# Stick-breaking attention: the later-key sums and the mask as single-pass products of exact constants with high and low parts of the softplus rows

## The chip, the cores and the metric

The kernel runs on one core of one Trainium2 chip. The metric is the device time of one execution in microseconds (us), taken as the median over runs of the same kernel. One launch computes the whole network; every weight is streamed once from the chip's main memory.

## What is computed

A batch of one sequence of 256 tokens with 1024 channels goes through twelve stages: an S5 and pooling mixer, a mixture of experts, stick-breaking attention, a second mixture of experts, and then eight stages of a second network (convolution, recurrent and latent-attention mixers, each followed by a feed-forward part). The change touches one stage, the stick-breaking attention with 16 heads of 64 channels:

```
z = (q @ k) * 64 ** -0.5
causal = key position < query position
log_keep = where(causal, log_sigmoid(-z), 0)
log_after = reverse_cumsum(log_keep over keys) - log_keep
wts = where(causal, exp(log_sigmoid(z) + log_after), 0)
out = wts @ v
```

Since log_sigmoid(-z) is minus softplus(z), and log_sigmoid(z) is z minus softplus(z), the logarithm of a weight is z minus the sum of the softplus over this key and all later allowed keys.

## The kernel before

**Layout of a head.** Keys lie on the 128 partitions and queries along the row. For 256 tokens a head needs 384 columns (`WIDE`): columns 0 to 255 are key tile 0 against all queries, columns 256 to 383 are key tile 1 against queries 128 to 255. One accumulation bank of TensorE holds them; four banks (`Q`) rotate over the heads.

**Work of head n.** `scores(n)` multiplies k and q in float32 into the bank (lines 1444 and 1445). ScalarE forms log(1 + exp(-|z|)) in three instructions (lines 1501 to 1503). VectorE adds max(z, 0), which gives the softplus row (line 1537), and multiplies its two diagonal 128x128 squares by a strict triangle, one instruction each (line 1539). `log_weights(n)` then adds onto the scores in the bank, by TensorE: a minus-triangle times the softplus for the sums inside a key tile, a minus-ones matrix times the softplus of key tile 1 for the queries of the second half, and the identity times a matrix of zeros and -1e30 on the two diagonal squares, which is the mask (lines 1454 to 1458). ScalarE takes the exponential of the bank (line 1508), and `values(n)` multiplies v by those weights (lines 1471 and 1472).

**float32 and fp32r products.** A product of float32 operands stands in the trace as two pairs of a weight load and a matmul; one of fp32r operands stands as one pair. The rest of the network uses fp32r with operands split into a rounded high part and the remainder, the low part (three products for one). The attention itself is computed in float32 throughout.

**Order on the engines.** It is written out by hand, the same loop on each engine for n = 0 to 17. TensorE does scores(n), log_weights(n-1), values(n-2). ScalarE does the three logarithm steps of n and then the exponential of n-1; every fourth head it also rounds a finished pair of output chunks (line 1319). VectorE does the softplus of n, and every fourth head the remainder of that pair (line 1323). The softplus rows and the logarithm rows have two buffers each. Each dependent step on VectorE waits for the one before it, by the helper `link`.

**Around the loop.** Before it TensorE computes q, k and v from the normalised input `x_hi`, `x_lo` (line 291 to 293 and 1421 to 1423) while ScalarE and VectorE split the streamed weight tiles into `w_hi` and `w_lo` (lines 267 and 274). The ring holds six tiles, of which four are split before a stage starts. After the loop `outer_pe` multiplies the attention's output by the output weights (lines 298 to 300). ScalarE copies q out of the banks at line 1490.

Of the kernel before, what the change touches and what calls it, by code (L numbers as in the profile page):

```python
# [17 lines left out]
T = 256  # L18
# [62 lines left out]
def unit_widths():  # L81
# [12 lines left out]
    "act": ["step", "start hi", "x_hi", "x squared", "rms seed", "seed", "c_hi",  # L94
            "silu", "h_hi", "router tanh", "ple tanh", "xg_hi", "y_hi",
            "dt", "mag", "sine", "uv", "pooled hi", "yg hi", "glu",
            "q", "log", "weights",
            "lam", "inner hi", "r", "i", "a", "root", "gelu",
            "latent squared", "latent seed", "latent q", "latent hi", "rotation", "head squared", "head seed", "exp", "turned copy"],
    "dve": ["step", "start lo", "x", "x_lo", "rms variance", "rstd", "rstd copy", "z", "variance", "c_lo",  # L100
# [44 lines left out]
def build(nc, dram, columns, stages, known):  # L145
    starts, n_tiles = stream_plan(stages)
    ctx = ExitStack()
    with ctx:
# [1260 lines left out]
        def token_product(pe, st, ks, xh, xl, name):  # L1409
# [15 lines left out]
            for i in range(4):  # L1425
                after(psum[i], ("dve", (name + " copy", st, i)))

        def sb_rows(h_):
            return slice(SB_DIM * (h_ % 2), SB_DIM * (h_ % 2) + SB_DIM)

        def sb_pe(pe, st):
            product(pe, 2 * KC, KC, x_hi, x_lo, lambda n: (psum[n // 2], bank(psum[n // 2])[:, n % 2, :]),
                    lambda n: ("qk", st, n // 2) if n % 2 else None, input_ready(pe, st))
            for f in range(8):
                after(psum[f], ("act", ("q", st, f)) if f < 4 else ("dve", ("k", st, f)))
            token_product(pe, st, KC, x_hi, x_lo, "v")

            def scores(h_):
                b, r, c = Q[h_ % 4], sb_rows(h_), h_ // 2
                before(pe, b)  # L1440
                if h_ == 0:
                    pe.wait_ge(act_did["q"], act_did.at("q", st, 3))
                    pe.wait_ge(dve_did["k"], dve_did.at("k", st, 7))
                nc.tensor.matmul(b[:, 0:T], sb_k[r, c, 0:P], sb_q[r, c, :], start=True, stop=True, skip_group_check=True)
                nc.tensor.matmul(b[:, T:WIDE], sb_k[r, c, P:T], sb_q[r, c, P:T], start=False, stop=True, skip_group_check=True).then_inc(
                    pe_did["scores"], pe_did.next("scores", st, h_))

            def log_weights(h_):

                b, soft = Q[h_ % 4], sb_soft[:, h_ % 2, :]  # L1450
                pe.wait_ge(dve_did["softplus"], dve_did.at("softplus", st, h_))
                pe.wait_ge(act_did["log"], act_did.at("log", st, h_))
                add = dict(start=False, stop=True, skip_group_check=True)
                nc.tensor.matmul(b[:, 0:T], column("minus_tri", 0, P), soft[:, 0:T], **add)
                nc.tensor.matmul(b[:, P:T], column("minus_ones", 0, P), soft[:, T:WIDE], **add)
                nc.tensor.matmul(b[:, T:WIDE], column("minus_tri", 0, P), soft[:, T:WIDE], **add)
                nc.tensor.matmul(b[:, 0:P], column("ident", 0, P), column("future", 0, P), **add)
                nc.tensor.matmul(b[:, T:WIDE], column("ident", 0, P), column("future", 0, P), **add).then_inc(
                    pe_did["log weights"], pe_did.next("log weights", st, h_))
                after(b, ("act", ("weights", st, h_)))  # L1460

            def values(h_):
                b, r, w = psum[4 + h_ // 4], sb_rows(h_), sb_w[:, h_ % 2, :]
                if h_ % 4 == 0:
                    before(pe, b)
                pe.wait_ge(act_did["weights"], act_did.at("weights", st, h_))
                if h_ == 0:
                    pe.wait_ge(dve_did["v copy"], dve_did.at("v copy", st, 3))
                out = bank(b)[r, h_ // 2 % 2, :]
                cols = slice(h_ * SB_DIM, (h_ + 1) * SB_DIM)  # L1470
                nc.tensor.matmul(out, sb_v[:, 0, cols], w[:, 0:T], start=True, stop=False, skip_group_check=True)
                nc.tensor.matmul(out[:, P:T], sb_v[:, 1, cols], w[:, T:WIDE], start=False, stop=True, skip_group_check=True).then_inc(
                    pe_did["values"], pe_did.next("values", st, h_))

            for n in range(SB_HEADS + 2):
                if n < SB_HEADS:
                    scores(n)
                if 0 < n <= SB_HEADS:
                    log_weights(n - 1)
                if n > 1:  # L1480
                    values(n - 2)
            for i in range(4):
                after(psum[4 + i], ("dve", ("c_lo", st, i)))
            outer_pe(pe, st, range(KC), 0, KC - 1)

        def sb_act(act, st):
            for f in range(4):
                split_hi(act)
                act.wait_ge(pe_did["qk"], pe_did.at("qk", st, f))
# [26 lines left out]
        def sb_dve(dve, st):  # L1516
# [14 lines left out]
            for n in range(SB_HEADS + 2):  # L1531
                if n < SB_HEADS:
# [2 lines left out]
                    if n > 1:  # L1535
                        dve.wait_ge(pe_did["log weights"], pe_did.at("log weights", st, n - 2))
                    link(dve, "dve", nc.vector.scalar_tensor_tensor(soft, Q[n % 4][:, 0:WIDE], 0.0, sb_log[:, n % 2, :], ALU.max, ALU.add))
                    for at in (0, T):
                        last = nc.vector.tensor_tensor(soft[:, at:at + P], soft[:, at:at + P], column("strict", 0, P), ALU.mult)
                    last.then_inc(dve_did["softplus"], dve_did.next("softplus", st, n))  # L1540
                if n > 1 and (n - 2) % 4 == 3:
                    i = (n - 2) // 4
                    rest_of_c(dve, st, i, bank(psum[4 + i]))
# [1276 lines left out]
```

## Time and profile before

| | |
|---|---|
| median of 3 runs | 2400.03 us (2397.57 to 2400.14) |
| profiled execution, its own time | 2397.32 us |
| its span, first to last instruction | 2395.5 us |
| mean granted TensorE clock | 0.960 of full speed |
| TensorE matmul busy | 2203.1 us, 92% |
| VectorE busy | 1555.4 us, 65% |
| ScalarE busy | 1199.7 us, 50% |
| attention loop, first logarithm to last values | about 670.8 to 726.5 us |

The profile is one execution. Busy time is that of the instructions of an engine; for TensorE the ends of matmuls are modelled, so that the distance between the starts of two matmuls says more than their durations. The two levels of the TensorE clock, 1.2 and 2.4 GHz, stand as 0.50 and 1.00.

### The profile page before, as it was taken

How to read it: one execution, taken by the hardware profiler on the slowest of the kernel's cores; microseconds unless marked ns; L12 is line 12 of the kernel's file. 1: busy time of each engine (PE TensorE's matmuls, PEld its weight loads, DVE VectorE, ACT ScalarE, POOL GpSimd, SP SyncE). 2: the span in 40 equal slices, each digit the busy share in tenths (PEclk: the TensorE clock that was granted, in tenths of full speed). 3: DMA queues.
4: the chain of work that ended last, by engine and by line, in shares of the span. 5: the costliest groups of instructions: out<-in, count | busy, mean ns of one | idle time of the engine just before them, and what ended most of it. 6: DMA issues, size and time to landing. Idle time of an engine off the chain costs nothing.

```text
span 2395.5 us, 29338 instructions
## 1 busy us (share of the span) xinstructions
PE 2203.1 (92%) x11070; PEld 1850.9 (77%) x11070; DVE 1555.4 (65%) x2061; ACT 1199.7 (50%) x1586; POOL 40.0 (2%) x41
## 2 busy tenths in 40 slices
PE   6479999997999999999799999599997999999999
PEld 5258888886977888787798888578875688888887
DVE  7977558888446656888875557855455555566554
ACT  3125447776354545777545444644444454445443
POOL 1220000000000000000000000000000000000000
PEclk9698999998999999999899999799998999999999
DMA  6023668997512566999555654345652355545663
GB/s 251 18 79 124 194 194 301 356 353 276 188 53 71 184 194 226 337 351 357 186 194 171 194 190 140 125 150 184 191 161 71 99 184 184 192 159 171 193 199 97
DMA packets 123005, 451.52 MB, mean 188 GB/s; under 512 B 13809, under 2 KB 13809, under 8 KB 121969
## 3 DMA queue, kind: packets, MB, share of 16 engines
q1 hardware_dynamic: 121536, 442.03, 55.0%
q0 software_dynamic: 1040, 6.82, 0.7%
q8 instruction: 88, 1.44, 0.2%
q10 hardware_dynamic: 288, 0.81, 0.1%
q14 instruction: 53, 0.43, 0.1%
HBM read 448.55 MB, written 1.05 MB: 188 GB/s over the span
## 4 chain that ended last, share of the span: by engine, by line
PE 78%; DVE 12%; ACT 3%; issue 3%; DMA 3%; POOL 1%; ACTq 0%; SPq 0%; DVEq 0%; POOLq 0%
PE bank L298 20%; PE bank L300 20%; PE bank L299 20%; DVE w_lo L274 4%; PE bank L291 3%; PE bank L292 3%; PE bank L293 3%; DMA raw<-in_stream 2%; ACT w_hi L267 1%; DVE scr L2382 1%; PE bank L611 1%; DVE scr L2366 1%; DVE scr L1652 1%; PE bank L1044 1%; PE bank L2192 1%
## 5 line engine op out<-in xcount | busy, mean ns | idle before, releaser
L274 DVE TENSOR_TENSOR w_lo<-raw,w_hi 128x1024 fp32r<-128x1024 f32 x839 | 1002.3, 1223 | 529.7 <-ACT w_hi L267 524.6
L267 ACT ACTIVATE w_hi<-raw 128x1024 fp32r<-128x1024 f32 x839 | 874.8, 1059 | 699.2 <-PE bank L300 535.6
L298 PE MATMUL bank<-w_hi,x_hi 128*128 128x512 f32 (+1 forms) x1056 | 414.7, 393 | 8.7 <-DVE x_lo L511 8.7
L300 PE MATMUL bank<-w_hi,x_lo 128*128 128x512 f32 (+1 forms) x1056 | 411.6, 390 | 0.0
L299 PE MATMUL bank<-w_lo,x_hi 128*128 128x512 f32 (+1 forms) x1056 | 411.6, 390 | 0.0
L298 PE MATMUL bank<-w_hi,c_hi 128*128 128x512 f32 x906 | 358.4, 396 | 55.3 <-issue 23.1
L300 PE MATMUL bank<-w_hi,c_lo 128*128 128x512 f32 x906 | 356.1, 393 | 0.0
L299 PE MATMUL bank<-w_lo,c_hi 128*128 128x512 f32 x906 | 356.1, 393 | 0.0
L298 PEld LDWEIGHTS bank<-w_hi,c_hi 128*128 128x128 f32 x906 | 172.2, 190 | 96.8 <-issue 51.3
L298 PEld LDWEIGHTS bank<-w_hi,x_hi 128*128 128x128 f32 x1056 | 199.9, 189 | 49.6 <-issue 5.6
L291 PE MATMUL bank<-x_hi,w_hi 128*128 128x256 f32 x736 | 212.3, 288 | 25.0 <-DVE w_lo L274 21.2
L300 PEld LDWEIGHTS bank<-w_hi,x_lo 128*128 128x128 f32 x1056 | 199.6, 189 | 41.2
L299 PEld LDWEIGHTS bank<-w_lo,x_hi 128*128 128x128 f32 x1056 | 199.9, 189 | 40.0
L292 PE MATMUL bank<-x_lo,w_hi 128*128 128x256 f32 x736 | 210.8, 286 | 0.0
L293 PE MATMUL bank<-x_hi,w_lo 128*128 128x256 f32 x736 | 210.7, 286 | 0.0
L300 PEld LDWEIGHTS bank<-w_hi,c_lo 128*128 128x128 f32 x906 | 172.0, 190 | 36.3
L299 PEld LDWEIGHTS bank<-w_lo,c_hi 128*128 128x128 f32 x906 | 172.2, 190 | 35.4
L291 PEld LDWEIGHTS bank<-x_hi,w_hi 128*128 128x128 f32 x736 | 144.2, 196 | 26.2 <-issue 21.2
L298 PE MATMUL bank<-w_hi,xg_hi 128*128 128x512 f32 x384 | 152.9, 398 | 6.8 <-DVE c_lo L1188 6.7
L300 PE MATMUL bank<-w_hi,xg_lo 128*128 128x512 f32 x384 | 150.1, 391 | 0.0
L299 PE MATMUL bank<-w_lo,xg_hi 128*128 128x512 f32 x384 | 149.9, 390 | 0.0
L292 PEld LDWEIGHTS bank<-x_lo,w_hi 128*128 128x128 f32 x736 | 144.3, 196 | 0.0
(398 smaller groups left out, 2096.1 us busy)
## 6 DMA issues: line engine op xcount, KB each, us to landing
raw<-in_stream SPq DMA_DIRECT2D x839, 512.0 KB, 4.4
ln_rows<-in_ln POOLq DMA_DIRECT2D x4, 1024.0 KB, 5.6
scr<-in_xt SPq DMA_DIRECT2D x1, 1024.0 KB, 5.4
scr<-in_s POOLq DMA_DIRECT2D x1, 1024.0 KB, 12.6
x<-in_x POOLq DMA_DIRECT2D x1, 1024.0 KB, 15.6
out_x<-x SPq DMA_DIRECT2D x4, 256.0 KB, 2.7
par<-in_par ACTq DMA_DIRECT2D x1, 765.5 KB, 9.6
scr<-in_ple POOLq DMA_DIRECT2D x1, 512.0 KB, 9.7
```

Source lines behind the costliest of these rows:

```text
L267: nc.scalar.activation(w_hi[:, n % RING, :], raw[:, n % RING, :], ACT.Copy).then_inc(hi_done, 1)
L274: nc.vector.tensor_tensor(w_lo[:, n % RING, :], raw[:, n % RING, :], w_hi[:, n % RING, :].bitcast(F32), ALU.subtract).then_inc(lo_done, 1)
L291: nc.tensor.matmul(out, hi, xh, start=start, stop=False, skip_group_check=shared)
L292: nc.tensor.matmul(out, hi, xl, start=False, stop=False, skip_group_check=shared)
L293: return nc.tensor.matmul(out, lo, xh, start=False, stop=stop, skip_group_check=shared)
L298: nc.tensor.matmul(out, xh, hi, start=start, stop=False)
L299: nc.tensor.matmul(out, xh, lo, start=False, stop=False)
L300: return nc.tensor.matmul(out, xl, hi, start=False, stop=stop)
L611: mm = nc.tensor.transpose(bank(H3[j])[:, c % 2, tokens(tt)], hidden[:, tt, c * P:(c + 1) * P], column("ident", 0, P))
L1044: mm = nc.tensor.transpose(at, hidden[:, tt, c * P:(c + 1) * P], column("ident", 0, P))
L1652: last = nc.vector.scalar_tensor_tensor(dst, src, w, dst, ALU.mult, ALU.add)
L2192: last = nc.tensor.matmul(bank(b)[rows, p // 2 % 2, :], c, s5_s[p % 2][q][:, n, :], start=(q == 0), stop=(q == 3), skip_group_check=True, ...
```

## The change

The softplus row of a head is split on VectorE into a high part rounded to fp32r and a low part that is the rest. The four constant matrices are copied once to fp32r (their entries are 0, plus or minus 1, and -1e30) by ScalarE at the start of the stage, with a wait of TensorE on it at head 0. `log_weights` then runs over the two parts with fp32r products: the minus-triangle on all 384 columns at once, the minus-ones on 128 columns, and one product of the identity with the mask for both diagonal squares, read by a repeated access pattern. The two strict-triangle multiplications on VectorE become one instruction over both squares. The high and low rows lie in `x_hi` and `x_lo`, which the stage has finished reading by then; the constants lie in chunks 8 and 9 of `c_hi`.

```diff
+        sb_soft_hi, sb_soft_lo = (ap[:, 0:3, :].rearrange("p a t -> p (a t)").rearrange("p (b w) -> p b w", b=2) for ap in (x_hi, x_lo))
+        sb_const = c_hi[:, 8:10, :].rearrange("p a t -> p (a t)").rearrange("p (n m) -> p n m", m=P)
+        SB_CONST = ("minus_tri", "minus_ones", "ident", "future")
+
+        def diagonal(ap):
+            return ap.rearrange("p (a m) -> p a m", m=P)[:, 0::2, :]
...
             def log_weights(h_):
-                b, soft = Q[h_ % 4], sb_soft[:, h_ % 2, :]
+                b = Q[h_ % 4]
+                if h_ == 0:
+                    pe.wait_ge(act_did["constants"], act_did.at("constants", st))
                 pe.wait_ge(dve_did["softplus"], dve_did.at("softplus", st, h_))
                 pe.wait_ge(act_did["log"], act_did.at("log", st, h_))
                 add = dict(start=False, stop=True, skip_group_check=True)
-                nc.tensor.matmul(b[:, 0:T], column("minus_tri", 0, P), soft[:, 0:T], **add)
-                nc.tensor.matmul(b[:, P:T], column("minus_ones", 0, P), soft[:, T:WIDE], **add)
-                nc.tensor.matmul(b[:, T:WIDE], column("minus_tri", 0, P), soft[:, T:WIDE], **add)
-                nc.tensor.matmul(b[:, 0:P], column("ident", 0, P), column("future", 0, P), **add)
-                nc.tensor.matmul(b[:, T:WIDE], column("ident", 0, P), column("future", 0, P), **add).then_inc(
+                minus_tri, minus_ones, ident, future = (sb_const[:, i, :] for i in range(4))
+                for soft in (sb_soft_hi[:, h_ % 2, :], sb_soft_lo[:, h_ % 2, :]):
+                    nc.tensor.matmul(b[:, 0:WIDE], minus_tri, soft, **add)
+                    nc.tensor.matmul(b[:, P:T], minus_ones, soft[:, T:WIDE], **add)
+                nc.tensor.matmul(diagonal(b[:, 0:WIDE]), ident, future.unsqueeze(1).to_broadcast([P, 2, P]), **add).then_inc(
                     pe_did["log weights"], pe_did.next("log weights", st, h_))
...
         def sb_act(act, st):
+            for i, name in enumerate(SB_CONST):
+                last = nc.scalar.activation(sb_const[:, i, :], column(name, 0, P), ACT.Copy)
+            last.then_inc(act_did["constants"], act_did.next("constants", st))
...
-                    for at in (0, T):
-                        last = nc.vector.tensor_tensor(soft[:, at:at + P], soft[:, at:at + P], column("strict", 0, P), ALU.mult)
-                    last.then_inc(dve_did["softplus"], dve_did.next("softplus", st, n))
+                    strict = column("strict", 0, P).unsqueeze(1).to_broadcast([P, 2, P])
+                    link(dve, "dve", nc.vector.tensor_tensor(diagonal(soft), diagonal(soft), strict, ALU.mult))
+                    hi, lo = sb_soft_hi[:, n % 2, :], sb_soft_lo[:, n % 2, :]
+                    link(dve, "dve", nc.vector.tensor_copy(hi, soft))
+                    nc.vector.tensor_tensor(lo, soft, hi.bitcast(F32), ALU.subtract).then_inc(dve_did["softplus"], dve_did.next("softplus", st, n))
```

## Rows read from the trace of the kernel before

**Rows 1.** The page's chain that ended last, share of the span by engine.

```profile
PE 78%; DVE 12%; ACT 3%; issue 3%; DMA 3%; POOL 1%; ACTq 0%; SPq 0%; DVEq 0%; POOLq 0%
```

**Rows 2.** Stretches of the attention loop: length, busy of each engine, PEclk, DMA.

```profile
674.00:682.00 8.00, 8.00 (x29) 6.33 (x28) 1.98 (x6) 2.51 (x5) 0.00 (x0) 0.53 0.08 34
692.00:702.00 10.00, 10.00 (x58) 7.84 (x57) 3.85 (x10) 6.11 (x14) 0.00 (x0) 1.00 0.00 0
```

**Rows 3.** Timeline, one head in the steady loop: start, duration, engine, line.

```profile
694.56 0.70 PE L1444 MATMUL bank<-scr 64*128 64x256 f32 x2
...
695.41 0.70 PE L1454 MATMUL bank<-scr,par 128*128 128x256 f32 x2
...
696.93 0.65 PE L1471 MATMUL bank<-scr 128*64 128x256 f32 x2
...
697.14 0.56 DVE L1537 SCALAR_TENSOR_TENSOR scr<-bank,scr 128x384 f32<-128x384 f32 x1 [2.08 <-ACT scr L1503]
...
697.72 0.70 PE L1444 MATMUL bank<-scr 64*128 64x256 f32 x2
697.74 0.49 DVE L1539 TENSOR_TENSOR scr<-scr,par 128x128 f32<-128x128 f32 x2
...
698.57 0.70 PE L1454 MATMUL bank<-scr,par 128*128 128x256 f32 x2
```

**Rows 4.** Timeline, the first heads of the loop.

```profile
672.39 0.56 DVE L1537 SCALAR_TENSOR_TENSOR scr<-bank,scr 128x384 f32<-128x384 f32 x1 [1.10 <-ACT scr L1503]
...
673.53 1.22 PE L1454 MATMUL bank<-scr,par 128*128 128x256 f32 x2 [4.38 <-DVE scr L1539]
...
676.39 1.22 PE L1444 MATMUL bank<-scr 64*128 64x256 f32 x2
...
680.82 0.95 PE L1471 MATMUL bank<-scr 128*64 128x256 f32 x2
...
681.92 0.70 PE L1444 MATMUL bank<-scr 64*128 64x256 f32 x2
```

**Rows 5.** Timeline, the last head and the product behind the loop.

```profile
722.43 0.56 DVE L1537 SCALAR_TENSOR_TENSOR scr<-bank,scr 128x384 f32<-128x384 f32 x1 [2.08 <-ACT scr L1503]
...
723.58 0.70 PE L1454 MATMUL bank<-scr,par 128*128 128x256 f32 x2 [0.49 <-DVE scr L1539]
...
725.10 0.65 PE L1471 MATMUL bank<-scr 128*64 128x256 f32 x2
...
726.54 0.50 PE L298 MATMUL bank<-w_hi,c_hi 128*128 128x512 f32 x1
```

**Rows 6.** Groups by line and shape on VectorE: count, busy us, mean ns.

```profile
L943 DVE TENSOR_TENSOR xg_lo<-bank,xg_hi 128x384 fp32r<-128x384 f32 x16 | 8.9, 556 | 1.7
...
L2349 DVE COPY scr<-small 128x256 f32<-128x256 f32 x4 | 0.9, 284 | 0.0
L1364 DVE TENSOR_TENSOR tmp_r<-rstd 128x256 f32<-128x256 f32 x2 | 0.9, 426 | 0.1
```

**Rows 7.** Timeline, single-pass products of 384 columns, the first after idle time.

```profile
225.02 0.44 PE L892 MATMUL bank<-c_lo,y_hi 128*128 128x384 f32 x1 [0.80 <-DVE x_lo L939]
225.30 0.34 PE L892 MATMUL bank<-c_lo,y_lo 128*128 128x384 f32 x1
225.48 0.35 PE L892 MATMUL bank<-c_lo,y_hi 128*128 128x384 f32 x1
```

**Rows 8.** Timeline, single-pass products of 32 and 16 columns at the low clock.

```profile
184.87 0.37 PE L787 MATMUL bank<-rw,x_hi 128*128 128x32 f32 x1
185.08 0.36 PE L788 MATMUL bank<-rw,x_lo 128*128 128x16 f32 x1
185.29 0.37 PE L787 MATMUL bank<-rw,x_hi 128*128 128x32 f32 x1
```

**Rows 9.** Timeline, ScalarE's first copy of q in the attention stage.

```profile
606.22 0.60 ACT L1490 ACTIVATE scr<-bank 128x512 f32<-128x512 f32 x1 [6.13 <-PE bank L293]
```

**Rows 10.** Stretches of the latent attention, columns as in rows 2.

```profile
1878.00:1881.00 3.00, 1.84 (x11) 1.27 (x11) 1.38 (x6) 2.24 (x6) 0.00 (x0) 1.00 0.56 175
...
1887.00:1890.00 3.00, 1.84 (x10) 1.13 (x9) 1.95 (x9) 1.29 (x5) 0.00 (x0) 0.96 0.56 175
```

More of the change, by code:

```diff
@@ L96 @@
             "dt", "mag", "sine", "uv", "pooled hi", "yg hi", "glu",
-            "q", "log", "weights",
+            "q", "log", "weights", "constants",
             "lam", "inner hi", "r", "i", "a", "root", "gelu",
```

## The prediction

> **What bounds the kernel now.** I read the page's chain of work first. It is 78% TensorE [rows 1], and TensorE's own products set the pace, so a microsecond taken from TensorE counts where nothing else is just behind it. Next I looked at the stretches of the attention loop. TensorE is busy 10.00 of 10 us, at the full clock, while VectorE is busy 3.85 and ScalarE 6.11; earlier, from 674 to 682, it is as busy at a mean clock of 0.53, that is nearly all at 1.2 GHz [rows 2]. So the loop looks bound by TensorE. The timeline of one head says by how much. From one start of the scores to the next are 697.72 - 694.56 = 3.16 us: scores 0.85, log_weights 1.52 (695.41 to 696.93), values 0.79 [rows 3].
>
> The second reading is the one that matters for this change: how far behind is the other path, from the scores of a head through ScalarE and VectorE back to TensorE? Scores to the start of the softplus takes 697.14 - 694.56 = 2.58 us [rows 3]. Softplus start to log_weights start, read at the last head where TensorE stands waiting, takes 723.58 - 722.43 = 1.15 us [rows 5]. In the written order, the scores of head n+2 come right behind log_weights(n) and values(n-1). So a loop through two heads closes: 2.58 + 1.15 + 1.52 + 0.79 = 6.04 us for two heads, 3.02 us a head. It is hidden behind 3.16 us of TensorE work by 0.14 us only. The reader should keep these two numbers, 3.16 and 3.02: the change shortens the first path a lot and hands work to the second.
>
> **TensorE's part of the change.** Ten pairs of load and matmul a head become five. A single-pass product of 384 columns is followed by the next after 225.48 - 225.30 = 0.18 us at full clock [rows 7]. A single-pass product of 128 columns is not in the trace. Products of 16 and 32 columns both take 0.21 us at 1.2 GHz [rows 8], so something other than the columns, of 256 cycles, sets the floor; at 2.4 GHz that is 0.11 us. I take 0.11 for 128 columns and 0.12 for the last product of 256. The sum is 0.18 + 0.11 + 0.18 + 0.11 + 0.12 = 0.70 us, 0.82 less than the 1.52 of before. Bounds: below, columns alone, 0.18 + 0.053 twice and 0.107, that is 0.57; above, if a short product took at the full clock the 0.21 us that it takes at the low one [rows 8], 0.90. If TensorE stood idle before them, the first takes 0.28 instead of 0.18 [rows 7]; so 0.80. At 1.2 GHz the sum is 0.32 + 0.21 + 0.32 + 0.21 + 0.21 = 1.27 us against 676.39 - 673.53 = 2.86 us before [rows 4].
>
> The Trainium skill prices short products lower: "TensorE: Matmul & The Clock Gate", section "Back-to-back issue gap", gives about 81 ns for each load and matmul pair of 128 columns. By it log_weights would be 0.06 us shorter than in my sum, 0.03 us a head on a path of two heads, some 0.4 us in all. No row shows a 128-column single-pass product, and the nearest rows stand at 107 ns, which I keep.
>
> **VectorE's part.** The softplus instruction of 0.56 us stays. Behind it, two masks of together 0.59 us with hand-overs (1.15 - 0.56) are replaced by three instructions one after another, each waiting for the one before. The mask of 256 elements: 0.43 us, as the 256-element product of two tensors. The copy of 384 elements inside on-chip memory: a copy of 256 took 284 ns; half a cycle more per element gives 0.35 us (128 x 0.52 ns = 67 ns); at a cycle per element, as the 384-element subtraction, it would be 0.56. The subtraction: 0.56 us [rows 6]. Hand-overs: 723.58 - 722.43 - 0.56 - 0.49 leaves 0.10 for two, so I take 0.03 each inside and 0.04 to TensorE: 0.13. Sum behind the softplus 1.34 + 0.13 = 1.47 us, 0.88 more than before. Upper bound: 1.09 more, with the slow copy. A lower one: hand-overs at nothing, 0.75 more.
>
> **The two together.** TensorE's own work falls to 0.85 + 0.70 + 0.79 = 2.34 us a head. The path through two heads becomes 2.58 + 1.15 + 0.88 + 0.80 + 0.79 = 6.20 us, 3.10 a head. So the loop goes from 3.16, bound by TensorE, to 3.10, bound by the path through VectorE: 0.82 us a head are taken from TensorE, and 0.06 arrive. TensorE stands idle for 3.10 - 2.44 = 0.66 us a head, in front of log_weights.
>
> **First heads.** Here TensorE is at 1.2 GHz and bound by itself, so more arrives. Before: log_weights(0) starts at 673.53, scores(3) at 681.92 [rows 4]. In between lie two log_weights of 2.86, scores(2) and values(0) (681.92 - 680.82 = 1.10), so scores is 8.39 - 5.72 - 1.10 = 1.57. After: log_weights(0) starts 0.88 later, at 674.41, takes 1.27 + 0.10, then scores(2) to 677.4, log_weights(1) to 678.6, values(0) to 679.8 (its softplus and weights are ready before). So scores(3) starts at 679.8, 2.1 us earlier. Its softplus starts 1.57 + (2.58 - 0.85) = 3.30 later, at 683.1, and log_weights(3) at 683.1 + 2.03 = 685.1; behind it 1.59 us to scores(5), at 686.7. Before, scores(5) starts at 681.92 + 2 x 3.16 = 688.24. The gain so far is 1.5 us. I let the clock rise at about 682, as before; if it rose at 679.5 another 1 us would come, and if two heads later the gain would fall by 1.
>
> **Steady heads.** From scores(5) to scores(15), ten heads at 0.06: 0.6 us.
>
> **End.** Scores(15) to log_weights(15) grows by 0.88 us, and since before TensorE waited there only 0.49 us, I count from scores to scores: before 723.58 - 719.84 (681.92 + 12 x 3.16) = 3.74, after 2.58 + 2.03 = 4.61, 0.87 more. Log_weights(15) takes 0.72 less with its first product after idle. The two values behind it, 726.54 - 725.10 = 1.44 us, stay [rows 5]. Loss 0.15 us.
>
> **Costs that I put at nothing.** The four constant copies on ScalarE come before the weight splits of the stage. A copy of 512 elements takes 0.60 us, so four of 128 take under 2.4; ScalarE then stands idle 6.13 us before the first copy of q [rows 9], and four of the ring's tiles are already split, so that absorbs it. Uncovered they would cost their 1 to 2 us once. Behind them in ScalarE's queue are only those splits, and behind these VectorE's remainders and the refills of the ring by SyncE, for tiles that TensorE takes up several microseconds later. TensorE's wait for the constants at head 0 is met some 70 us before. Every fourth head VectorE has 0.69 us more (line 1323); softplus work of 2.03 us plus this is 2.72, under 3.10, so it fits, by 0.4 us. Nothing is moved past a DMA; the loop moves almost no data [rows 2].
>
> **Sum.** -1.5 - 0.6 + 0.15 = -1.95 us. The profiled execution took 2397.32 us by itself, 1.8 more than its span, and lies 2.7 under the median of 2400.03; I subtract from the median: 2398.0 us. A change under 0.2% (4.8 us) cannot be told from none here.
>
> **Rival 1, TensorE's saving arrives in full.** If VectorE's chain hid behind TensorE, ten heads and the last would give 0.82 each and the first two 1.6 each: 9.0 + 3.2, or 2388 us. For it: TensorE is busy all the time in the loop [rows 2]. Against: the path of 3.02 us is only 0.14 behind, and log_weights itself waits for the lengthened chain. It decides only if ScalarE's and VectorE's steps took 1.5 us less than the rows say. Chance 6%.
>
> **Rival 2, the chain is longer than I sum.** The copy at a cycle per element (+0.21) and the short products at 0.21 (+0.20) make 6.61 us for two heads, 3.30 a head: +0.14 against before instead of -0.06, so 13 heads turn by 0.2 each, 2.6 us: 2400.6 us. Nothing in the trace speaks for the slow copy but that the output is rounded. Chance 21%.
>
> **Rival 3, the clock falls, and the kernel gets slower.** In the loop of before TensorE has no gaps; after, it is idle a fifth of the time. In the latent attention three microseconds with TensorE busy 1.84 kept the clock at 1.00, and nine microseconds on, a stretch just as busy shows 0.96, the start of a fall [rows 10]. So such gaps can be survived and need not be. At 1.2 GHz a head would take 1.57 + 1.27 + 1.10 = 3.94 us, busy throughout, 0.84 more than 3.10. If it lasts for all twelve steady heads that is +10 us: 2408 us, slower by 0.3%. It passes 0.2% from eight slow heads on; since TensorE is full again once slow, falls should be repaired within a few heads, each costing some 2 us. The Trainium skill speaks for this rival: "TensorE: Matmul & The Clock Gate", section "A second HAM failure mode: psum-queue depth-cycling", tells of a kernel whose short idle times between groups of matmuls make the clock swing. The rows above show one such fall and one such hold. Chance 8% for a loop mostly slow.
>
> **How the numbers follow.** My forecast has 65%, the rivals 6, 21 and 8%. The range: below, the forecast with a quick rise of the clock (-1), the low bounds (hand-overs -0.13 and log_weights -0.13, that is 0.13 a head, 1.6 us) reaches 2395; above, rival 2 with two short falls of the clock reaches 2403. Faster by over 0.2% is rival 1 and a little of the low end, 8%; slower is rival 3 and a little of repeated falls, 8%; the same 84%.
>
> **What would show it.** The profile after should show TensorE idle about 0.6 us before log_weights, released by VectorE's subtraction; VectorE's copy at 0.35 us; starts of single-pass products 0.18 and 0.11 apart; 3.10 us from scores to scores; the loop's end 2 us earlier, and all else shifted as a block. Wrong would be: a wait of VectorE for TensorE, a copy of 0.56 us, a clock under 1.00 between 683 and 722, or a stage outside the loop that changes its length.

## The result, and the profile after

| | before | after |
|---|---|---|
| median of 4 runs each | 2398.8 us | 2419.61 us (2414.22 to 2424.62) |
| ratio, 95% interval | | 1.0089 (1.0064 to 1.0113) |
| profiled execution: own time, span | 2397.32, 2395.5 us | 2414.22, 2412.4 us |
| loop: start of ScalarE's table load to the first output product | 669.46 to 726.54: 57.08 us | 668.52 to 744.32: 75.80 us |
| mean granted TensorE clock | 0.960 | 0.947 |

The kernel became slower by 0.9%; 2398.0 us was predicted. The loop alone grew by 18.72 us. Everything ahead of it took 0.94 us less and everything behind it 0.88 us less, which makes the 16.9 us of the spans. So the cause is inside the loop. The profiled execution after is the fastest of its four, and no trace shows where the slower ones spend the rest of the 20.8 us between the medians. "Loop" below always means the stretch of the table's last line, which for every kernel is read in its own profiled execution. Outside the loop the seventeen profiled executions of this document take 2336.6 to 2350.4 us, so a difference of 1 to 3 us inside the loop need not show in a median.

The chain of work still names TensorE, one point higher than in [rows 1]:

```profile
PE 79%; DVE 12%; ACT 3%; DMA 3%; issue 3%; POOL 1%; ACTq 0%; SPq 0%; DVEq 0%; POOLq 0%
```

Stretches of the loop after, columns as in [rows 2]: length, busy of PE, PEld, DVE, ACT, POOL, PEclk, DMA.

```profile
674.00:682.00 8.00, 8.00 (x25) 6.01 (x24) 3.20 (x7) 3.05 (x7) 0.00 (x0) 0.50 0.02 6
692.00:702.00 10.00, 10.00 (x29) 6.96 (x29) 4.94 (x10) 5.34 (x11) 0.00 (x0) 0.50 0.01 2
712.00:722.00 10.00, 10.00 (x29) 7.08 (x29) 5.20 (x11) 4.61 (x9) 0.00 (x0) 0.50 0.00 0
732.00:742.00 10.00, 9.32 (x29) 6.73 (x27) 3.85 (x9) 4.01 (x8) 0.00 (x0) 0.50 0.00 1
744.00:748.00 4.00, 4.00 (x17) 3.10 (x16) 0.69 (x1) 0.95 (x2) 0.00 (x0) 0.90 0.02 4
```

Here is the whole loss in one column. In [rows 2] the clock stands at 1.00 from 692 to 702; after, it stands at 0.50 from the first log_weights on, and rises only at about 744.8, when the output products have just begun. TensorE is nevertheless busy 10.00 of 10 us. Its count of matmuls is halved (29 against 58): part of this is the change (five products where there were ten matmuls), part the clock.

One head in the middle of the loop, timeline of TensorE and VectorE, to hold against [rows 3]:

```profile
698.24 1.22 PE L1451 MATMUL bank<-scr 64*128 64x256 f32 x2
...
699.81 0.69 PE L1465 MATMUL bank<-x_hi,c_hi 128*128 128x384 f32 x1
...
700.30 0.31 PE L1466 MATMUL bank<-x_hi,c_hi 128*128 128x128 f32 x1
...
700.40 0.63 PE L1465 MATMUL bank<-x_lo,c_hi 128*128 128x384 f32 x1
...
700.83 0.31 PE L1466 MATMUL bank<-x_lo,c_hi 128*128 128x128 f32 x1
...
700.94 0.52 PE L1467 MATMUL bank<-c_hi 128*128 128x256 f32 x1
...
701.39 1.12 PE L1480 MATMUL bank<-scr 128*64 128x256 f32 x2
...
702.86 1.22 PE L1451 MATMUL bank<-scr 64*128 64x256 f32 x2
...
703.00 0.56 DVE L1554 TENSOR_TENSOR x_lo<-scr,x_hi 128x384 fp32r<-128x384 f32 x1
...
704.44 0.69 PE L1465 MATMUL bank<-x_hi,c_hi 128*128 128x384 f32 x1
```

A head takes 702.86 - 698.24 = 4.62 us: scores 1.57, log_weights 1.58, values 1.47. Nothing waits: the subtraction of the next head ends at 703.56, and log_weights takes it up at 704.44. TensorE is the bound again, at half its clock. 16 heads make the account: from scores(3) to scores(15), twelve heads, 55.52 us (679.73 to 735.25 in the timeline) against 37.92 before, 17.60 more. The first heads are 1.25 shorter (679.73 - 668.52 against 681.92 - 669.46), the end 2.37 longer (744.32 - 735.25 against 726.54 - 719.84). Together 18.72.

The entry and the end of the loop, timeline, to hold against [rows 4, 5]:

```profile
673.55 0.66 PE L1465 MATMUL bank<-x_hi,c_hi 128*128 128x384 f32 x1 [5.34 <-DVE x_lo L1554]
...
740.62 0.69 PE L1465 MATMUL bank<-x_hi,c_hi 128*128 128x384 f32 x1 [0.68 <-DVE x_lo L1554]
...
744.32 0.71 PE L298 MATMUL bank<-w_hi,c_hi 128*128 128x512 f32 x1
```

And the groups of VectorE's chain, whose sizes [rows 6] were to give, and of the constants on ScalarE:

```profile
L1554 DVE TENSOR_TENSOR x_lo<-scr,x_hi 128x384 fp32r<-128x384 f32 x16 | 8.9, 558 | 0.6
L1549 DVE SCALAR_TENSOR_TENSOR scr<-bank,scr 128x384 f32<-128x384 f32 x16 | 8.9, 557 | 36.1 <-ACT scr L1515 36.1
L1551 DVE TENSOR_TENSOR scr<-scr,par 128x256 f32<-128x256 f32 x16 | 6.8, 424 | 0.6
L1553 DVE CAST x_hi<-scr 128x384 fp32r<-128x384 f32 x16 | 5.7, 359 | 0.6
...
L1497 ACT ACTIVATE c_hi<-par 128x128 fp32r<-128x128 f32 x4 | 0.9, 298 | 0.0
```

Mask 0.42, copy 0.36, subtraction 0.56 us: as predicted to 0.01.

### The profile page after: what moved, and what is told of

Read it like the earlier page. It is cut to its first block, busy times and chain, and to the rows that moved or that the text cites. A ratio compares the mean times of both kernels' runs of the same rounds, so it can differ in the third digit from the quotient of the medians.

```text
span 2412.4 us, 29198 instructions
## 1 busy us (share of the span) xinstructions
PE 2220.0 (92%) x10990; PEld 1859.9 (77%) x10990; DVE 1568.9 (65%) x2077; ACT 1201.4 (50%) x1590; POOL 40.1 (2%) x41
## 4 chain that ended last, share of the span: by engine, by line
PE 79%; DVE 12%; ACT 3%; DMA 3%; issue 3%; POOL 1%; ACTq 0%; SPq 0%; DVEq 0%; POOLq 0%
PE bank L298 20%; PE bank L300 20%; PE bank L299 20%; DVE w_lo L274 4%; PE bank L291 3%; PE bank L292 3%; PE bank L293 3%; DMA raw<-in_stream 2%; ACT w_hi L267 1%; DVE scr L2396 1%; PE bank L611 1%; DVE scr L2380 1%; PE bank L1451 1%; PE bank L1465 1%; PE bank L1480 1%
```

## The experiments

In all of them a "filler" is an fp32r product of 512 columns whose output is overwritten before anything reads it. It reads the constants, and in the kernel before, which has none, `x_hi`. Where the text says "new products" it means the single-pass ones of the change, and "old products" the float32 ones of before. The diffs are cut to the lines that matter.

**1 and 2. The clock handed over at full speed.** Before and after alike, the clock has fallen when log_weights(0) begins, because TensorE waits 4.4 us (before) or 5.3 us (after) for the first softplus. Here 24 fillers cover this wait, once in the changed kernel (start_filled_new) and once in the kernel before (start_filled_old).

```diff
+            def fill(count):
+                for _ in range(count):
+                    nc.tensor.matmul(psum[7][:, :], sb_const[:, 0, :], c_hi[:, 8:10, :].rearrange("p a t -> p (a t)"), start=True, stop=True, skip_group_check=True)
             for n in range(SB_HEADS + 2):
                 if n < SB_HEADS:
                     scores(n)
+                if n == 1:
+                    pe.wait_ge(act_did["constants"], act_did.at("constants", st))
+                    fill(24)
```

> The changed kernel with 24 products of 512 columns (fp32r, into a bank not yet in use) behind scores(1), so that TensorE works through its wait for the first softplus (some 5.2 us) and enters the loop at 2.4 GHz. The output is unchanged. Theory A (the loss is only the way in: at the low clock the loop never gets out, at the high clock it would stay): clock 1.00 through the loop, 3.1 us a head by the path over VectorE, loop some 49 us from log_weights(0), time about 2394 us. Theory B (the mix of products cannot hold the clock): it falls within some heads, back to 4.63 us a head, 2414 to 2420 us. Theory C (the longer chain is what costs): TensorE idle and well over 3.1 us a head at the full clock.

> The kernel before with the same 24 products in the same place. The output is unchanged. All theories: the 8 us at 1.2 GHz at the head of the loop go. From log_weights(0) to scores(3) took 8.39 us, at the full clock it is 3.16 x 2 + 1.52 - ... = about 5.5 us; so about -2.8 us, 2396 us. It is the measure for the filled start of the changed kernel.

New products: 2413.16 us (2410.55 to 2418.33), ratio 1.0055 (1.0038 to 1.0071), loop 72.71. Old ones: 2398.89 us, 1.0 (0.999 to 1.0009), loop 54.41, clock 1.00 throughout. The loop became 2.67 us shorter, as expected; the time did not. So a full clock at the entry stays with the old products and is soon gone with the new. Timeline and stretches of start_filled_new where it falls:

```profile
682.28 0.70 PE L1451 MATMUL bank<-scr 64*128 64x256 f32 x2
...
684.32 0.44 PE L1465 MATMUL bank<-x_hi,c_hi 128*128 128x384 f32 x1 [1.13 <-DVE x_lo L1561]
...
686.42 1.22 PE L1451 MATMUL bank<-scr 64*128 64x256 f32 x2
```

```profile
680.00:684.00 4.00, 3.19 (x17) 2.27 (x15) 2.17 (x5) 2.92 (x7) 0.00 (x0) 1.00 0.00 0
684.00:688.00 4.00, 3.68 (x13) 2.53 (x14) 2.17 (x5) 1.30 (x3) 0.00 (x0) 0.69 0.00 0
```

TensorE waited 1.13 us for the subtraction of head 2 and was at 1.2 GHz from 685.5 on (the mean of 0.69 puts it there), 1.2 us after the wait, to the end of the loop.

**3 and 4. The two halves of the change apart.** long_chain_old_products keeps VectorE's new chain (mask, copy, subtraction) and gives TensorE back its five float32 products. short_chain_new_products does the reverse: VectorE writes the row rounded and leaves out copy and subtraction, and log_weights reads this high row twice, so that the sums are doubled and the output is not the reference's.

```diff
# long_chain_old_products, in log_weights
+                soft = sb_soft[:, h_ % 2, :]
+                nc.tensor.matmul(b[:, 0:T], column("minus_tri", 0, P), soft[:, 0:T], **add)
...
# short_chain_new_products, on VectorE and in log_weights
-                    link(dve, "dve", nc.vector.scalar_tensor_tensor(soft, Q[n % 4][:, 0:WIDE], 0.0, sb_log[:, n % 2, :], ALU.max, ALU.add))
+                    link(dve, "dve", nc.vector.scalar_tensor_tensor(hi, Q[n % 4][:, 0:WIDE], 0.0, sb_log[:, n % 2, :], ALU.max, ALU.add))
...
-                    link(dve, "dve", nc.vector.tensor_copy(hi, soft))
-                    nc.vector.tensor_tensor(lo, soft, hi.bitcast(F32), ALU.subtract)
...
-                for soft in (sb_soft_hi[:, h_ % 2, :], sb_soft_lo[:, h_ % 2, :]):
+                for soft in (sb_soft_hi[:, h_ % 2, :], sb_soft_hi[:, h_ % 2, :]):
```

> The VectorE and ScalarE side of the change alone: high and low part are made, but log_weights reads the float32 row with the five float32 products of before. The output is that of before. Theory A and B (clock by the new products): clock 1.00 from about 682, the path of two heads is (2.58 + 2.03 + 1.52 + 0.79) / 2 = 3.46 us a head, 0.30 more than before on 12 heads and 1.8 at both ends: about 2404 us. Theory C: most of the 20 us are here already, 2415 us or more. A clock that stays low here would put the fall on the waits, not on the products.

> The TensorE side of the change with a short chain: the softplus is written rounded, masked in place, and log_weights reads this high row twice; copy and subtraction are left out, so the sums are doubled and the output is not the reference's. TensorE's instructions are those of the changed kernel. Chain behind the softplus about 1.05 us instead of 2.03. Theory B and A (TensorE at 1.2 GHz sets the pace, fully busy): 4.63 us a head as in the changed kernel, first head 1 us earlier, about 2418 us. Theory C: the loss goes, 2400 us or less.

Long chain, old products: 2405.07 us (2401.97 to 2406.65), ratio 1.0019 (1.001 to 1.0029), loop 60.80. The clock rises at about 679.5 and stays, with a wait in every second head:

```profile
683.70 0.70 PE L1464 MATMUL bank<-scr,par 128*128 128x256 f32 x2 [0.57 <-DVE x_lo L1555]
...
690.66 0.70 PE L1464 MATMUL bank<-scr,par 128*128 128x256 f32 x2 [0.56 <-DVE x_lo L1555]
```

Two heads take 690.66 - 683.70 = 6.96 us. This is the path of the prediction with the old log_weights in it: 2.58 + 1.15 + 0.88 + 1.52 + 0.79 = 6.92. Short chain, new products: 2417.95 us (2415.71 to 2418.5), ratio 1.0076 (1.0059 to 1.0093), loop 73.98, the clock at 1.2 GHz all through it and TensorE never idle. Its middle, as a stretch:

```profile
700.00:710.00 10.00, 10.00 (x29) 7.11 (x29) 1.97 (x4) 4.01 (x8) 0.00 (x0) 0.50 0.01 2
```

So the chain, taken alone, costs 4 to 6 us (3.7 in the loop, 6.2 between the medians); the loss of 20 needs the new products, and they cause it without the long chain too.

The clock comes back at the end of this loop a moment before the output products. Timeline and stretch:

```profile
744.34 0.55 PE L1481 MATMUL bank<-scr 128*64 128x128 f32 x2
744.82 0.50 PE L298 MATMUL bank<-w_hi,c_hi 128*128 128x512 f32 x1
```

```profile
744.60:744.80 0.20, 0.20 (x2) 0.00 (x0) 0.00 (x0) 0.00 (x0) 0.00 (x0) 0.82 0.00 0
```

In front of the rise lie the last log_weights and values(14) and values(15) in a row, a stretch that differs from the loop in that no scores stand in it.

**5 to 7. The clock held up by fillers.** Three fillers in front of every log_weights from the second on, into the bank that the next scores takes: with the 24 at the start (start_and_heads_filled), without them (heads_filled), and without them over half the array, with a stationary operand of 128 rows and 64 columns, `sb_const[:, 0, 0:64]` (heads_filled_half).

```diff
+            def fill_head(n):
+                b = Q[(n + 1) % 4]
+                before(pe, b)
+                for _ in range(3):
+                    nc.tensor.matmul(b[:, :], sb_const[:, 0, :], c_hi[:, 8:10, :].rearrange("p a t -> p (a t)"), start=True, stop=True, skip_group_check=True)
...
+                if 1 < n <= SB_HEADS:
+                    fill_head(n)
                 if 0 < n <= SB_HEADS:
                     log_weights(n - 1)
```

> The changed kernel with the 24 products at the start and three further products of 512 columns (fp32r, 128 rows by 128 columns of the array) in each head, in front of log_weights, in a bank whose content is overwritten next. The output is unchanged. Theory B (the mix of products and gaps cannot hold the clock; filled gaps would): clock 1.00 through the loop; the path over VectorE then sets 3.10 us a head, or TensorE's own 2.4 + 0.7 = 3.1: loop 53 to 55 us from table load to the output product, against 57.1 before and 75.8 in the changed kernel; about 2396 to 2399 us. Rival D (products of this form cannot hold the clock whatever the gaps): 4.63 + 1.28 = 5.9 us a head, about 2440 us.

> As the run beside it without the 24 products at the start: the loop is entered at 1.2 GHz. The output is unchanged. Theory B: with the fillers the clock rises within two or three heads; loop 57 to 61 us, 2399 to 2403 us. If it stays at 0.50, a loop at 1.2 GHz is not got out of by more full products either: 5.9 us a head, 2440 us.

> As heads_filled, but each filler uses a stationary operand of 64 columns instead of 128, as the products of values do; just as many columns stream through. The output is unchanged. If the clock goes by how long columns stream, it rises as in heads_filled, 2399 to 2403 us. If it goes by how much of the array works, it rises later or not at all, up to 2440 us.

2396.87 us (ratio 0.9998, 0.9988 to 1.0007), 2401.66 us (1.0012, 1.0001 to 1.0024) and 2401.4 us (1.0008, 0.9999 to 1.0018); loops 54.92, 57.79 and 56.73. The 45 to 69 more products make the changed kernel 18 to 23 us faster. Without the start fillers the clock rises at 682.5 with the whole array and at 682.1 with half of it, 2.0 and 1.4 us behind the end of the first three.

**8. Fewer, longer float32 products.** To ask whether the number of products matters: the kernel before with its five float32 products merged into three (384, 128 and 256 columns) and one mask on VectorE.

```diff
-                nc.tensor.matmul(b[:, 0:T], column("minus_tri", 0, P), soft[:, 0:T], **add)
+                nc.tensor.matmul(b[:, 0:WIDE], column("minus_tri", 0, P), soft, **add)
...
-                nc.tensor.matmul(b[:, T:WIDE], column("minus_tri", 0, P), soft[:, T:WIDE], **add)
-                nc.tensor.matmul(b[:, 0:P], column("ident", 0, P), column("future", 0, P), **add)
-                nc.tensor.matmul(b[:, T:WIDE], column("ident", 0, P), column("future", 0, P), **add).then_inc(
+                future = column("future", 0, P).unsqueeze(1).to_broadcast([P, 2, P])
+                nc.tensor.matmul(diagonal(b[:, 0:WIDE]), column("ident", 0, P), future, **add).then_inc(
```

> The part of the change that costs VectorE nothing: float32 products as before, but the minus-triangle over all 384 columns at once and the mask of both squares in one product, three products instead of five, and the two strict masks in one VectorE instruction. No split, no constants. The output is unchanged. As many columns stream in the float32 passes as before, so the clock should rise at the same place by every theory. log_weights 1.52 -> some 1.4 us, chain behind the softplus 1.15 -> 1.02: 3.04 us a head by TensorE: -0.12 us a head, about -2 us in all, 2397 us; at most the slope of a tie.

2398.6 us, ratio 0.9996 (0.9984 to 1.0008), loop 57.00, 3.14 us a head where 3.04 was expected. The clock rises here, 8.7 us behind the start of log_weights(0) against 8.0 before. So merging alone doesn't keep it down; the step to single-pass products does.

**9. Short chain, filled at the start.** Number 4 with the 24 fillers; the low part is left out here too.

> short_chain_new_products with the 24 products at the start: TensorE enters at 2.4 GHz, the chain is 1 us shorter, so that it hardly waits in the loop; as there, the high row is used twice and copy and subtraction are left out, so the sums are doubled. It tells the gaps from the mix. If the clock fell in start_filled_new because of the gaps (0.6 us a head): it stays at 1.00 here, some 2.6 us a head by the path (2.58 + 1.05 + 0.78 + 0.79 over two heads), loop about 47 us, 2388 us. If the mix of products alone is too thin for the clock: it falls here too, 4.6 us a head, loop about 71 us, 2413 us.

2388.25 us (2386.43 to 2389.35), ratio 0.9957 (0.9941 to 0.9974), loop 46.55, clock 1.00 throughout. The same mix of products that stayed at 1.2 GHz in number 4 stays at 2.4 GHz here, 2.67 us a head with waits of 0.21 us in every second head. The loop is 10.5 us shorter than before, 2.67 of them by the full clock at the entry alone (number 2). The median reaches the 2388 us of rival 1, but not by its sum: a head gains 0.49 us, not 0.82. It takes both, the entry at full clock and no split on VectorE.

**10 and 11. Two fillers a head, and one.** As number 5, to find where the waits begin to cost the clock.

> start_and_heads_filled with two fillers a head instead of three. The output is unchanged. TensorE's own work is then 3.23 - 0.23 = 3.0 us a head, under the 3.10 of the path over VectorE. If the clock holds, the timeline shows 3.10 to 3.15 us a head with a wait for VectorE's subtraction, loop 53.4 us against 54.9, about 2395 us. If it falls, 5.4 us a head and over 2420 us.

> The same with one filler a head. The output is unchanged. If the clock holds, the same 3.10 to 3.15 us a head as with two, since the path sets it. It held with three and fell with none (start_filled_new); I expect it to fall at some point of the loop here, 2400 to 2420 us.

2397.93 us (0.9993 to 1.0013) and 2396.9 us (0.9989 to 1.0013), loops 53.97 and 53.74, clock 1.00 in both. With one a head TensorE waits in every second head and keeps the clock; the fall that I expected there did not come:

```profile
700.46 0.44 PE L1465 MATMUL bank<-x_hi,c_hi 128*128 128x384 f32 x1 [0.52 <-DVE x_lo L1569]
...
703.32 0.36 PE L1465 MATMUL bank<-x_hi,c_hi 128*128 128x384 f32 x1
```

**12. Fillers up to the eighth head, none behind.** `if 1 < n <= 8` in number 5: filled and unfilled heads in one loop.

> The changed kernel with 24 products of 512 columns behind scores(1) and three in front of each log_weights up to the eighth, none after it, so one loop holds both kinds of heads. If the waits of the longer chain between the thinner products are what lets the clock go, TensorE keeps 2.4 GHz and 3.2 us a head up to scores(8), near 693 us, falls to 1.2 GHz within some 6 us of it, as it did behind the start fillers alone, and goes on at 4.63 us a head: eight heads at 1.4 us more than in the fully filled loop, some 66 us of loop instead of 54.9, median about 2408 us. If a loop once warm and in its rhythm holds the clock by itself, so that only the first heads needed help, it stays at 1.00 with 3.17 us a head and waits of about 0.6 us for the subtraction: a loop of 54 us and a median of 2397 us.

2399.57 us (ratio 0.9998, 0.9986 to 1.0009). My theory, that the waits between the thinner products lose the clock, failed here: seven unfilled heads, each with a wait, kept it. Timeline of two of them, and the stretch around the last wait:

```profile
709.45 0.70 PE L1451 MATMUL bank<-scr 64*128 64x256 f32 x2
710.88 0.44 PE L1465 MATMUL bank<-x_hi,c_hi 128*128 128x384 f32 x1 [0.51 <-DVE x_lo L1569]
...
712.56 0.70 PE L1451 MATMUL bank<-scr 64*128 64x256 f32 x2
714.10 0.44 PE L1465 MATMUL bank<-x_hi,c_hi 128*128 128x384 f32 x1 [0.62 <-DVE x_lo L1569]
...
715.78 0.70 PE L1451 MATMUL bank<-scr 64*128 64x256 f32 x2
```

```profile
726.00:728.00 2.00, 1.23 (x5) 1.24 (x5) 0.68 (x2) 0.00 (x0) 0.00 (x0) 0.61 0.00 0
```

These are the two heads of the prediction, 715.78 - 709.45 = 6.33 us, 3.17 a head, with TensorE waiting 0.51 and 0.62 us for the subtraction. The clock falls only at about 726.4, within the last head's wait of 1.48 us. (The loop of this profiled execution is 55.94 us; its own time, 2408.06, is the longest of ten, by what lies outside the loop.) That left a new suspicion: not the many short waits, but a single longer one, such as the 1.13 us of number 1.

**13 to 15. The single longer wait.** Start fillers and three in front of log_weights(1) and (2) only (`if n in (2, 3)`), which covers that one wait; three fillers once (`if n == 2`), which raises the clock but leaves a wait behind it; three each in heads 2 to 4 (`if 1 < n <= 4`), its counterpart with the wait covered.

> The changed kernel with 24 products of 512 columns behind scores(1), three in front of log_weights(1), three in front of log_weights(2), and none after. Against the kernel filled at the start alone this covers only the one wait of 1.13 us in front of log_weights(2); the later heads wait about 0.6 us each, as they did in the kernel filled up to the eighth head. If that single longer wait is what let the clock go, TensorE keeps 2.4 GHz to the last head at 3.17 us a head, a loop of 54 to 56 us and a median near 2398 us. If unfilled heads this early let it go too (the 0.6 us waits, or their share of the time), it falls by about 690 and the loop takes some 70 us, median near 2412 us.

> The changed kernel with three products of 512 columns in front of log_weights(1), the only ones added. The clock stands at 1.2 GHz when they come; in the kernel with three in every head it rose right behind these first three, so it should rise at about 682 to 683 here too. Then log_weights(3) comes 4.65 us behind scores(3) while TensorE has 3.3 us of work, a wait of about 1.4 us. If a single wait of over a microsecond lets the clock go, it falls at about 688 and stays at 1.2 GHz, 4.63 us a head: a loop of some 74 us and a median near 2414 us. If only the wait for the first softplus, 5.3 us long, can do that, the clock holds: a loop of 57 us, median near 2400 us.

> As the kernel with three products once, but with three each in front of log_weights(1), (2) and (3), which covers the long wait; nothing behind the third. By the single long wait as cause: clock up at about 682, held to the last head at 3.17 us a head, a loop of 57 to 58 us, median near 2400 us. By any rule under which the thin heads that wait 0.6 us lose the clock: a fall by 695 and a loop of 68 us or more, median over 2410 us.

2397.21 us (0.9994, 0.9984 to 1.0004), 2410.22 us (1.0046, 1.0031 to 1.0061) and 2399.27 us (1.0004, 0.9993 to 1.0015); loops 54.21, 63.18 and 56.85. The first and third held 2.4 GHz to the end at 3.17 us a head, as expected. In the second, three products raised the clock, and what came then, timeline and stretches of three_products_once:

```profile
705.68 0.44 PE L1465 MATMUL bank<-x_hi,c_hi 128*128 128x384 f32 x1 [1.20 <-DVE x_lo L1562]
...
712.01 0.44 PE L1465 MATMUL bank<-x_hi,c_hi 128*128 128x384 f32 x1 [1.20 <-DVE x_lo L1562]
714.72 1.22 PE L1451 MATMUL bank<-scr 64*128 64x256 f32 x2
...
719.34 1.22 PE L1451 MATMUL bank<-scr 64*128 64x256 f32 x2
```

```profile
702.00:712.00 10.00, 7.62 (x39) 5.57 (x39) 6.23 (x13) 7.42 (x16) 0.00 (x0) 1.00 0.00 0
712.00:722.00 10.00, 9.98 (x30) 7.28 (x31) 4.50 (x9) 4.49 (x9) 0.00 (x0) 0.52 0.00 0
```

Here the loop settles in another rhythm with the same period: one wait of 1.20 us in two heads in place of 0.51 and 0.62. Four such waits left the clock up, the fifth, before 712.01, was followed by the fall, at about 712.4. Neither of the two expected outcomes came, a fall at about 688 or none. Its eight runs lie from 2404.2 to 2413.25 us, and the mean clock of each goes with its time (0.956 for the fastest, 0.950 for the slowest), which suggests that the moment of the fall differs from run to run; the trace is of one of the fastest, 2404.27 us. The last head of number 13 waited 1.35 us and that of number 15 1.48 us, and both kept the clock:

```profile
724.36 0.44 PE L1465 MATMUL bank<-x_hi,c_hi 128*128 128x384 f32 x1 [1.48 <-DVE x_lo L1562]
```

So a wait of 1.1 to 1.5 us among the new products may or may not be followed by a fall (it was in numbers 1, 12 and, at the fifth, 14; it was not in 13 and 15), and no wait of up to 0.63 us was.

## Why the prediction was wrong

The loop in this table is that of the one profiled execution, the median that of all runs.

| kernel with the new products | clock at the entry | longest wait in it, last head apart, us | clock in the loop | loop, us | median, us |
|---|---|---|---|---|---|
| after | low | none | low to the end | 75.80 | 2419.61 |
| 4, short chain | low | none | low to the end | 73.98 | 2417.95 |
| 1, filled at the start | full | 1.13 | falls behind that wait | 72.71 | 2413.16 |
| 14, three products once | low, raised | 1.20, every second head | full from 681.7, falls at 712.4 | 63.18 | 2410.22 |
| 12, filled to head 8 | full | 0.62 | full to the last head | 55.94 | 2399.57 |
| 15, heads 2 to 4 filled | low, raised | 0.63 | full | 56.85 | 2399.27 |
| 13, start and two heads filled | full | 0.63 | full | 54.21 | 2397.21 |
| 9, short chain, filled at the start | full | 0.21 | full | 46.55 | 2388.25 |

**The bound before and the path behind it: right.** The path through VectorE was computed as 3.02 us a head, hidden behind 3.16. Number 3 lengthened the path alone, and two heads took 6.96 us where the same sum gives 6.92.

**The new period: the mechanism right, the size off by 0.07, and the gain gone with it.** 3.10 us a head was predicted, 3.17 measured in numbers 12, 13 and 15. That is 0.01 above the 3.16 of before, so the 0.6 us that the steady heads were to give would not have come even at the full clock. From scores to log_weights of the same head 714.10 - 709.45 = 4.65 us against 4.61. The rest is log_weights itself: at the full clock behind a wait it takes 0.88 us (700.46 to 701.34 in number 11) against 0.80. The single terms were off both ways. The 128-column product takes 0.06 us, half of my 0.11; the 384-column product behind it 0.22 instead of 0.18, and the mask 0.26 instead of 0.12. The Trainium skill, "TensorE: Matmul & The Clock Gate", section "Back-to-back issue gap", has two figures: about 81 ns for a pair of 128 columns, which the prediction cites, and for a single matmul at the full clock its columns at 2.4 GHz plus 2.5 ns. For the 128-column product the trace agrees with the second (0.06 us, estimate 0.056); for the 384-column product behind it it doesn't (0.22 us, estimate 0.16). My floor of 256 cycles, read from [rows 8], was wrong for 128 columns.

**"I let the clock rise at about 682, as before": the step that failed.** [rows 2] showed TensorE busy 8.00 of 8 us at a mean clock of 0.53, with the rise at its end, and [rows 4] which products ran there: float32 ones, two pairs of load and matmul each. I read the rise as something that comes a time after the wait. It came from those products. With single-pass ones TensorE shows busy all the same and the clock does not rise in 70 us, with the long chain (after) or without (number 4). That the products are the cause is shown from both sides: the old ones with the new chain rise at 679.5 (number 3), merged float32 ones rise (number 8), and three products of 512 columns, 1.45 us of work, raise it in the new loop (numbers 6, 14 and 15). The traces are one of each kernel, but the other runs go with them: a mean clock of 0.944 to 0.948 in all four runs after, 0.946 to 0.948 in those of number 4, and 0.960 to 0.962 in the ten of number 3. What about the mix the clock goes by, no run isolates. "float32 products raise it" would say too much: scores and values are float32 in the new loop as well, and did not raise it in any head of these two loops, while the end of number 4, with values but no scores, did.

**Rival 3 had the right place and the wrong price.** It has the new loop at 1.2 GHz, for a fall. It put a slow head at 3.94 us; 4.62 was measured. Of the 0.68 missing, 0.31 are log_weights at the low clock, 1.58 instead of 1.27: the first 384-column product takes 0.49 and the second 0.43 instead of 0.32, the mask 0.45 instead of 0.21, and the short ones 0.10 and 0.11 instead of 0.21. And 0.37 are the values, 1.47 instead of 1.10: the 1.10 was read from 680.82 to 681.92 in [rows 4], where the clock was already rising. And it said that falls "should be repaired within a few heads", since TensorE is full when it is slow. That is the same failed step: being full did not repair anything. The Trainium skill's "TensorE: Matmul & The Clock Gate", section "A second HAM failure mode: psum-queue depth-cycling", which the rival named, tells of short idle times that make the clock swing; number 1 and number 14 show a fall behind such idle time, though no swing back within the loop's heads; the changed kernel itself has no idle time to swing by, so its loss is not of that kind.

**With the clock held, the time comes near 2398.0 us, but not by the forecast's sum.** A loop of 57.08 - 1.95 = 55.1 us was predicted. The changed kernel with nine fillers, entered at the low clock like the one before (number 15), takes 2399.27 us with a loop of 56.85, that is 0.23 less than before. Filled at the start and in two heads (number 13) it takes 2397.21 us with a loop of 54.21, that is 0.20 less than the 54.41 of the old products filled at the start (number 2). So even with its clock the change gains nothing that can be measured, and that these times lie within 1.3 us of the forecast says little, since the kernel before lies as near. TensorE's saving of 0.8 us a head is taken by VectorE's split; without the split 0.49 of it arrive (number 9, 2388.25 us). No version that keeps both parts of the softplus was measurably faster than the kernel before.

**Left open.** Why one wait of 1.1 to 1.5 us is followed by a fall and another is not; only one trace of each kernel was read. What raised the clock at the end of number 4, just ahead of the output products. And whether a mix of products between the old and the new would raise the clock unaided.

## What to carry to other kernels

Before putting fewer or thinner matmuls into a stretch that enters at the low clock, ask which products raise the clock there now, and whether the new ones have been seen to do it; a TensorE that shows busy 10 of 10 us may stay at 1.2 GHz. Read a rise of the clock as an effect of the work in front of it and never as an appointment in time, and price a low-clock stretch from rows that lie wholly at the low clock. If a thin loop must be entered at the low clock, a few wide products at its start can be worth trying: here nine of them, 1.45 us for three at the low clock, took the loop from 75.80 to 56.85 us. The one longer wait of the first heads was covered with them in the kernels that held the clock; where it was left (numbers 1 and 14), the clock fell there or later. Here this only won back what the change had lost.

## What the hardware showed that was not expected

- The same sequence of products, without idle time, ran a whole loop of 16 heads at 1.2 GHz when entered at 1.2 (number 4, 2417.95 us) and, with waits of 0.21 us, at 2.4 GHz when entered at 2.4 (number 9, 2388.25 us).
- Three products of 512 columns, 1.45 us of TensorE's time, were followed by the rise to 2.4 GHz within 1.3 to 2.3 us of their end (numbers 6, 14 and 15). At the full clock such products were nearly free where TensorE would have waited: with three in each head the loop took 54.92 us (number 5), with three in two heads only 54.21 (number 13).
- From start to start, an fp32r product of 128 columns takes 0.06 us at 2.4 and 0.11 at 1.2 GHz, and the product of 384 columns behind it 0.22 and 0.43, against 0.18 at 2.4 GHz behind one of its own width; so a short product's saving is partly paid by the next.
